# The last expert's scatter accumulates in PSUM on sums loaded there, and the norm chain reads the banks

## What is computed

```python
out = jnp.zeros((T + 1, D), jnp.float32).at[slot_tok].add(ys.astype(jnp.float32) * slot_gate[:, None])   # moe_ffn: 32 experts, 4 per token
...
x = x + gt2 * rms_norm(y, g_post_ffn[l])            # end of first_block
...
y = x * rsqrt(mean(x * x) + EPS) * norm_mix_gain    # start of second_block, rmsnorm
proj = y @ w_in_2
```

## Time and profile before

| | us |
|---|---|
| median of 3 runs | 2637.76 |
| lowest, highest run | 2636.64, 2644.43 |
| profiled execution, its span | 2643.0 |
| TensorE granted clock, mean | 0.979 |
| PE busy | 2496.3 (94%) |
| DVE busy | 1329.3 (50%) |
| ACT busy | 913.3 (35%) |
| GpSimd busy | 261.3 (10%) |

### The profile page before, as it was taken

One profiled execution on the slowest core, in us unless ns is written; L12 is line 12 of the kernel. 1 busy time (PEld: TensorE's weight loads), 2 busy tenths in 40 slices (PEclk: granted clock), 3 DMA queues, 4 the chain that ended last, 5 costly groups with the idle time before them and its releaser, 6 DMA issues.

```text
span 2643.0 us, 39144 instructions
## 1 busy us (share of the span) xinstructions
PE 2496.3 (94%) x16618; PEld 1762.0 (67%) x16618; DVE 1329.3 (50%) x1846; ACT 913.3 (35%) x1243; POOL 261.3 (10%) x181
## 2 busy tenths in 40 slices
PE   7988999999989999879999999999999999999998
PEld 5652323333323333278899899998899999887997
DVE  4451222212223222188777755756665765785755
ACT  4441111111111111056555544553444444435443
POOL 3000000000000000021000101262011201202200
PEclk9999999999999999989999999999999999999999
DMA  9689999999999999953455566555466466451562
GB/s 335 212 311 425 427 428 406 427 428 427 428 423 414 427 428 428 427 182 132 152 199 192 183 207 208 178 172 191 163 223 208 159 208 207 136 171 38 177 210 103
DMA packets 248986, 713.68 MB, mean 270 GB/s; under 512 B 12563, under 2 KB 186345, under 8 KB 223910
## 3 DMA queue, kind: packets, MB, share of 16 engines
q1 hardware_dynamic: 237424, 690.26, 68.8%
q10 hardware_dynamic: 9446, 15.97, 1.8%
q0 software_dynamic: 1936, 4.87, 0.6%
HBM read 710.01 MB, written 1.05 MB: 269 GB/s over the span
## 4 chain that ended last, share of the span: by engine, by line
PE 51%; DVE 3%; ACT 2%; issue 1%; POOL 0%; DVEq 0%; ACTq 0%; POOLq 0%
PE bank L429 19%; PE bank L671 13%; PE bank L434 10%; PE bank L623 4%; PE bank L703 2%; ACT ap L3945 1%; PE bank L899 1%; PE bank L2680 1%; PE bank L3456 0%; PE bank L467 0%; DVE stats L3219 0%; DVE xa L3217 0%; PE bank L4025 0%; ACT hi L362 0%; PE bank L3759 0%
## 5 line engine op out<-in xcount | busy, mean ns | idle before, releaser
L371 DVE TENSOR_TENSOR lo<-ring,hi 128x2048 fp32r<-128x2048 f32 x251 | 601.8, 2403 | 249.1 <-ACT hi L362 248.8
L362 ACT ACTIVATE hi<-ring 128x2048 fp32r<-128x2048 f32 x251 | 476.0, 1900 | 136.3 <-PE bank L671 106.8
L2130 PE MATMUL bank<-expert,xg 128*64 128x512 f32 x1664 | 387.6, 604 | 29.0 <-DMA expert<-in_w_mlp 28.1
L429 PE MATMUL bank<-x_hi,hi 128*128 128x256 f32 (+1 forms) x1576 | 369.1, 279 | 0.0
L429 PE MATMUL bank<-x_lo,hi 128*128 128x256 f32 (+1 forms) x1576 | 366.7, 278 | 0.0
L429 PEld LDWEIGHTS bank<-x_hi,hi 128*128 128x128 f32 (+1 forms) x1576 | 296.1, 188 | 3.3 <-issue 1.8
L429 PEld LDWEIGHTS bank<-x_lo,hi 128*128 128x128 f32 (+1 forms) x1576 | 296.0, 188 | 2.2 <-issue 0.7
L2130 PEld LDWEIGHTS bank<-expert,xg 128*64 128x64 f32 x1664 | 114.0, 137 | 241.7 <-issue 208.0
L2260 DVE TENSOR_TENSOR acc<-bank,acc 128x512 f32<-128x512 f32 x100 | 62.1, 683 | 332.7 <-PE bank L2238 332.6
L434 PE MATMUL bank<-x_hi,lo 128*128 128x256 f32 (+1 forms) x1576 | 197.0, 278 | 0.9 <-DVE lo L371 0.9
L2213 PE MATMUL bank<-expert,aT 128*64 128x512 f32 x832 | 185.7, 596 | 5.5 <-DMA expert<-in_w_mlp 5.5
(11 more groups left out here) (697 smaller groups left out, 3908.5 us busy)
## 6 DMA issues: line engine op xcount, KB each, us to landing
expert<-in_w_mlp SPq DMA_DIRECT2D x192, 2048.0 KB, 18.9
ring<-in_l_ffn_w_in SPq DMA_DIRECT2D x88, 1024.0 KB, 5.1
ring<-in_l_ffn_w_out SPq DMA_DIRECT2D x44, 1024.0 KB, 4.9
ring<-in_w_ada SPq DMA_DIRECT2D x24, 1024.0 KB, 7.0
ring<-in_l_gm_w_in SPq DMA_DIRECT2D x24, 1024.0 KB, 5.2
ring<-in_ffn_w_up SPq DMA_DIRECT2D x22, 1024.0 KB, 5.1
ring<-in_w_in SPq DMA_DIRECT2D x21, 1024.0 KB, 7.4
ring<-in_l_gm_w_out SPq DMA_DIRECT2D x12, 1024.0 KB, 4.9
```

The costliest lines, as they stand in the source:

```text
L362: e.activation(k.half("hi", u), k.slot(j), ACT.Copy).then_inc(*k.up("hi_done"))
L371: e.tensor_tensor(k.half("lo", u), k.slot(k.units[u][0]), k.half("hi", u).bitcast(F32), SUB).then_inc(*k.up("lo_done"))
L429: e.matmul(o, l, r, start=fresh, stop=False, skip_group_check=True)
L2130: i = e.matmul(banks[n][j][h * CAP:(h + 1) * CAP, :], x, W[:, (2 * h + j) * 512:(2 * h + j + 1) * 512], start=c == 0, stop=False, skip_gro ...
```

## The change

- In the 33rd place the addition of expert 30 to `acc` is marked quarter by quarter. Between the two halves of expert 31's second product PE now multiplies the identity by the four quarters of `acc`, 128x128 by 128x512 in fp32, each into a bank of its own (`sums_begin_pe`).
- Expert 31's scatter adds to these banks (`sums_end_pe`). Its eight products go in two sides of four, the left 256 columns of each bank and then the right ones, with a wait of PE for its own left side between them.
- DVE's four additions L2248, its statistics and products, GpSimd's two products and a DVE memset go away. `chain_act` and `chain_dve` do the norm from the four banks, in both engines' programs behind the branch past the overflow.
- The waits of ACT and DVE for PE's end of the experts stand behind the chain, and no longer ahead of it.
- In the overflow body the addition goes to the banks, through a scratch tile `s_out`.

```diff
--- before.py
+++ after.py
@@ -2246,9 +2246,6 @@
             av = k.t["acc"][:, :, q * 256:(q + 1) * 256]
             e.wait_ge(*k.mm("back", n, q))
             e.tensor_tensor(av, two(k.got("back", n, q)[:, :]), av, ADD).then_inc(*k.DVE(frees=("back", n, q)))
-            if key and q % 2:
-                for b in range(2):
-                    k.mark("dve_done", *key, b, q // 2)
         return
     for b in range(2):
         for h in range(2):
@@ -2258,6 +2255,32 @@
                 e.tensor_copy(av, bank).then_inc(*k.DVE(frees=("back", n, b, h)))
             else:
                 e.tensor_tensor(av, bank, av, ADD).then_inc(*k.DVE(*((*key, b, h) if key else ()), frees=("back", n, b, h)))
+
+
+def sums_begin_pe(k, e):
+
+    for b, h in quarters():
+        bank = k.bank(e, "sum", "acc", b, h, hold=True)
+        e.wait_ge(*k.dve("acc", b, h))
+        e.matmul(bank[:, :], k.cc("ident"), quarter(k.t["acc"], b, h), start=True, stop=False, skip_group_check=True)
+
+
+def sums_end_pe(k, e):
+
+    t, n = k.t, OF[NE - 1][0]
+    e.wait_ge(*k.act("Y", n))
+    for side in range(2):
+        if side:
+            e.wait_ge(*k.mm("sum", "left", 1, 1))
+        for b, h in quarters():
+            rows = slice((2 * h + side) * 32, (2 * h + side + 1) * 32)
+            e.matmul(k.got("sum", "acc", b, h)[:, side * 256:(side + 1) * 256], t[f"G{n % 5}"][rows, b * 128:(b + 1) * 128], t[f"Y{n % 3}"][rows, 0:256],
+                     start=False, stop=True, skip_group_check=True).then_inc(*k.MM("sum", "acc" if side else "left", b, h))
+    acc_free(k, "sum")
+
+
+def sum_bank(k, b, h):
+    return k.got("sum", "acc", b, h)[:, :]
 
 
 SMALL_AT = 18
@@ -2297,6 +2320,8 @@
         if p >= 1:
             downs = {n: k.bank(e, "down", n, hold=True) for n in OF[p - 1]}
             for i in range(2):
+                if i and p == NE:
+                    sums_begin_pe(k, e)
                 down_pe(k, e, p - 1, i, downs)
             for n in OF[p - 1]:
                 k.release("down", n)
@@ -2305,8 +2330,7 @@
                 for j in range(UPS[n]):
                     k.release("up", n, j)
     past = over_count(k, e)
-    for n in OF[NE - 1]:
-        scatter_pe(k, e, n)
+    sums_end_pe(k, e)
     for flag in PE_:
         k.mark(flag, "meet", "experts")
     return past
@@ -2349,7 +2373,7 @@
                 mark_dve(k, e, n)
         if p >= 2:
             for n in OF[p - 2]:
-                scatter_dve(k, e, n)
+                scatter_dve(k, e, n, *(("acc",) if p == NE else ()))
         if p == LATE_AT:
             turned_dve(k, e)
         if p == B2_AT:
@@ -2359,7 +2383,6 @@
                 gate_dve(k, e, n)
         if p == SMALL_AT:
             small2_dve(k, e)
-    e.memset(k.t["moments"][:, :, 2:3], EPS).then_inc(*k.DVE())
     k.mark("dve_done", "meet", "experts")
     return over_count(k, e)
 
...
@@ -2477,7 +2499,6 @@
                     e.wait_ge(*k.at("slow_dve_done", x, h, j, "x"))
                     e.activation(t["s_th"], t["s_x"], ACT.Tanh, scale=0.851).then_inc(*k.up("slow_act_done", x, h, j))
         e.wait_ge(*k.at("slow_dve_done", NE - 1, "down", 1, 1))
-    met(k, e, "experts", of=PE_)
     k.past("act", "overflow")
 
 
...
+    k.past("dve", "overflow")
+
+
+def moe_out_act(k, e):
+    chain_act(k, e, "post2", lambda b, h: sum_bank(k, b, h), lambda b, h: k.mm("sum", "acc", b, h), "mix2")
     met(k, e, "experts", of=PE_)
-    k.past("dve", "overflow")
-
-
-def moe_out_act(k, e):
-
-    t, mv = k.t, k.t["moments"]
-    e.activation(t["warm"], k.cc("ident")[:, 0:1], ACT.Sqrt).then_inc(*k.ACT())
-    for b in range(2):
-        e.wait_ge(*k.dve("post2", "var", b))
-        e.activation(mv[:, b, 1:2], mv[:, b, 1:2], ACT.Sqrt, bias=mv[:, b, 2:3]).then_inc(*k.ACT("post2", "std", b))
-    k.mark("act_done", "meet", "post2")
-    rms_squares_act(k, e, "mix2", lambda b, h: k.dve("post2", "x", b, h))
-    met(k, e, "post2")
-
-
-def moe_scaled(k, e, b, h, inc):
-    e.tensor_tensor(quarter(k.t["unit"], b, h), quarter(k.t["acc"], b, h), k.t["g2"][:, h * 512:(h + 1) * 512], MUL).then_inc(*inc)
-
-
-def moe_out_pool(k, e):
+
+
+def moe_out_dve(k, e):
+    e.wait_ge(*k.pool("g2", "done"))
+    chain_dve(k, e, "post2", lambda b, h: sum_bank(k, b, h), k.t["g2"], "mix2", lambda b, h: ("sum", "acc", b, h))
     met(k, e, "experts", of=PE_)
-    for h in range(2):
-        e.wait_ge(*k.dve("acc", 1, h))
-        moe_scaled(k, e, 1, h, k.POOL("post2", "scaled", h))
-
-
-def moe_out_dve(k, e):
-
-    t, mv, acc, st = k.t, k.t["moments"], k.t["acc"], k.t["post2_stats"]
-
-    def stats(b, h):
-        e.bn_stats(st[:, b, h, :], quarter(acc, b, h)).then_inc(*k.DVE())
-
-    def mean_square(b):
-        e.wait_ge(*k.dve())
-        e.bn_aggr(mv[:, b, 0:2], st[:, b, :, :].rearrange("p a b -> p (a b)")).then_inc(*k.DVE())
-        e.wait_ge(*k.dve())
-        e.scalar_tensor_tensor(mv[:, b, 1:2], mv[:, b, 0:1], mv[:, b, 0:1], mv[:, b, 1:2], MUL, ADD).then_inc(*k.DVE("post2", "var", b))
-
-    def add(b):
-        inverse_dve(k, e, "post2", b)
-        e.wait_ge(*k.dve())
-        for h in range(2):
-            if b:
-                e.wait_ge(*k.pool("post2", "scaled", h))
-            e.scalar_tensor_tensor(quarter(t["xa"], b, h), quarter(t["unit"], b, h), mv[:, b, 1:2], quarter(t["xa"], b, h), MUL, ADD).then_inc(*k.DVE("post2", "x", b, h))
-
-    for n in OF[NE - 1]:
-        scatter_dve(k, e, n, "acc")
-    e.wait_ge(*k.dve())
-    for b in range(2):
-        for h in range(2):
-            stats(b, h)
-        mean_square(b)
-    e.wait_ge(*k.pool("g2", "done"))
-    for h in range(2):
-        moe_scaled(k, e, 0, h, k.DVE())
-    for b in range(2):
-        add(b)
-    meet(k, e, DVE_, "post2")
-    square_dve(k, e, "mix2", 0)
-    rms_unit_dve(k, e, "mix2", 0)
-    square_dve(k, e, "mix2", 1)
-    rms_unit_dve(k, e, "mix2", 1)
 
 
 def lay_moe(k, c):
...
@@ -4270,7 +4240,6 @@
     meet(k, e, POOL_, "post1")
     late_gate_pool(k, e)
     meet(k, e, POOL_, "experts")
-    moe_out_pool(k, e)
     meet(k, e, POOL_, "post2")
     e.wait_ge(*k.dve("mix2", "unit", 1, 1))
     decay_pool(k, e, "hg", k.t["hD"])
```

More of the change, by code:

```diff
@@ L2431, in over_banks @@
 def over_banks(k):
-    n = OF[NE - 1][0]
-    back = {k.of["back", n, q] for q in range(4)}
-    return [k.ps[i] for i in range(8) if i not in back]
+    sums = {k.of["sum", "acc", b, h] for b, h in quarters()}
+    return [k.ps[i] for i in range(8) if i not in sums]
 def overflow_pe(k, e, past):
@@ L2513, in overflow_dve @@
                 for b in range(2):
-                    av = t["acc"][:, b, hf * 512:(hf + 1) * 512]
+                    av = sum_bank(k, b, hf)
                     e.wait_ge(*k.at("slow_mm_done", x, "down", hf, b))
-                    e.scalar_tensor_tensor(av, ps[2 + b][:, :], t["gov"][:, b, x:x + 1], av, MUL, ADD).then_inc(*k.up("slow_dve_done", x, "down", hf, b))
+                    e.wait_ge(*k.at("slow_dve_done"))
+                    e.tensor_scalar(t["s_out"], ps[2 + b][:, :], t["gov"][:, b, x:x + 1], None, MUL).then_inc(*k.up("slow_dve_done"))
@@ L2517, in overflow_dve @@
+                    e.wait_ge(*k.at("slow_dve_done"))
+                    e.tensor_tensor(av, av, t["s_out"], ADD).then_inc(*k.up("slow_dve_done", x, "down", hf, b))
         e.wait_ge(*k.at("slow_dve_done", NE - 1, "down", 1, 1))
-    met(k, e, "experts", of=PE_)
     k.past("dve", "overflow")
 def moe_out_act(k, e):
-    t, mv = k.t, k.t["moments"]
-    e.activation(t["warm"], k.cc("ident")[:, 0:1], ACT.Sqrt).then_inc(*k.ACT())
-    for b in range(2):
-        e.wait_ge(*k.dve("post2", "var", b))
-        e.activation(mv[:, b, 1:2], mv[:, b, 1:2], ACT.Sqrt, bias=mv[:, b, 2:3]).then_inc(*k.ACT("post2", "std", b))
@@ L2573, in moe_out_dve @@
-    e.wait_ge(*k.pool("g2", "done"))
-    for h in range(2):
-        moe_scaled(k, e, 0, h, k.DVE())
-    for b in range(2):
-        add(b)
-    meet(k, e, DVE_, "post2")
-    square_dve(k, e, "mix2", 0)
-    rms_unit_dve(k, e, "mix2", 0)
-    square_dve(k, e, "mix2", 1)
-    rms_unit_dve(k, e, "mix2", 1)
+    e.wait_ge(*k.pool("g2", "done"))
+    chain_dve(k, e, "post2", lambda b, h: sum_bank(k, b, h), k.t["g2"], "mix2", lambda b, h: ("sum", "acc", b, h))
+    met(k, e, "experts", of=PE_)
 def lay_moe(k, c):
@@ L2614, in lay_moe @@
             k.t[f"ab{i}"], k.t[f"Y{i}"] = share[:, i * 1024:i * 1024 + 512], share[:, i * 1024 + 512:(i + 1) * 1024]
-        bi("post2_stats", 128, 2, 2, 6)
         k.t["s_act"] = share[:, 0:2048].rearrange("p (a b) -> p a b", a=KC)
-        k.t["s_x"], k.t["s_th"] = share[:, 2048:2304], share[:, 2304:2560]
+        k.t["s_x"], k.t["s_th"], k.t["s_out"] = share[:, 2048:2304], share[:, 2304:2560], share[:, 2560:3072]
 RG = (("rg_w_r_2", "BD0", "r", 15), ("rg_w_i_2", "BD1", "ig", 18))
```

## The result

Over 20 runs each the changed kernel takes 2642.17 us in the median and the kernel before 2636.80. The ratio is 1.0018, with a 95% interval from 1.0011 to 1.0026: slower by 0.18%, 4.7 us of 2637, within the 0.3% that I had set as the limit of "the same". The profiled execution of the changed kernel spans 2641.7 us. Single executions of either kernel lie several us beside their median (2631.33 to 2645.14 before, 2638.18 to 2645.03 after), as much as the effect; so what follows compares places inside the traces, all counted from one event, the start of the first half of expert 31's second product (L2209; 1122.75 us before, 1120.29 after). It comes ahead of the new products; over all fourteen traces, of either kernel, it lies between 1119.2 and 1123.1, so times counted from the program's start would mix in up to 4 us of spread from before the seam.

A forecast was written before the change was run, and what follows sets the result against it. PE's work and the holes in it bound the kernel, so the turning's start decides. The late copy of 1.5 us and what follows came to +4.2, plus 0.1 for waits: +4.3, 2642.0 us; own range 2640.5 to 2643.5.

The forecast's parts named there:

- Where the bound lies: At the turning (L467): its start decides, and everything behind it, PE-bound from 1150 on, moves with it.
- The sums are loaded, +1.5: PE between the halves of expert 31's second product: four identity products take 3.4 us, delaying the second half 1.5 us.
- The scatter in two sides, 1.9: Expert 31's scatter on PE: first bank whole 1.9 us after its start, costing nothing if ACT comes later.
- ACT's place, the stall of 4.9: ACT behind its overflow branch: a 4.9 us stall, then the table load, puts the first square at 1137.2.
- The chain, 9.15: Second norm from the banks: 9.15 us from first square to turning, putting the turning 4.2 us later.
- What is removed: DVE's additions and statistics and GpSimd's products: already counted in DVE's 11.80 us; GpSimd's going saves nothing more.
- DVE branches as before: DVE's overflow branch: unchanged; before, its 6.2 us stall was covered by the wait for the last weights.
- The first rival: ACT is ready when the banks are: turning 0.6 us sooner, time 2637.2 us; chance 0.12.
- My rival on the other side: ACT stalls a second time between branch and squares: another 4.9 us, +9.2 in all, 2647.0 us; chance 0.04.
- The clock: PE's return to full clock moves with the work, costing nothing; rival, one stretch late: +1.7 us, 2643.7; chance 0.08.
- The waits moved, +0.1: ACT between its root and the weight splits: two more waits add 0.1 us, bounds 0 and 0.24.
- The sum: Whole kernel: +4.2 and +0.1 give +4.3 us, median from 2637.76 to 2642.0 us, 0.16% more.

The follow-up runs named there:

- e11: Changed kernel without the overflow on any engine and without the four products of the identity; one run, no ratio given, turning at +17.3 us.
- e7: Changed kernel without the overflow on any engine (its branches, loads of the count and body left out); 0.9990 of the kernel before.
- e1: Changed kernel with ACT's load of the count, its branch and its part of the overflow left out; 1.0009 of the kernel before.
- e4: Changed kernel with ACT's branch ahead of its last copy, which stands in both paths; 1.0009 of the kernel before.
- e8: Changed kernel with only DVE's branch and its part of the overflow left out; one run, no ratio given, turning at +24.8 us.
- e12: The changed kernel itself measured once more; 1.0018 of the kernel before.
- e3: Changed kernel with the small activation that loads the Sqrt table moved ahead of ACT's load of the count and branch; 1.0031 of the kernel before.
- e10: Kernel before with ACT's first weight split moved into its hole ahead of the second norm's squares; 0.9990 of the kernel before.
- e5: Changed kernel with ACT's branch ahead of its last copy and DVE's ahead of the addition of expert 30, both kept in both paths; 1.0009 of the kernel before.
- e2: Kernel before with ACT's load of the count and its branch left out; 0.9995 of the kernel before.

## Why the prediction was right, point by point

*Where the bound lies.* Right: the start of the turning decides, and what is behind it follows at its distance (gain 4.5 us behind, both before and after).

*The sums are loaded, +1.5.* Measured 1.78 in the profile (5.50 - 3.72), and 2.1 between e11 and e7. From the first of the four products to the second half passed 3.64 us (1125.79 - 1122.15), against 3.4, and they began 0.1 us later than I had put them: my term was small by 0.3.

*The scatter in two sides, 1.9.* Measured 1.96 in e1. It cost nothing in the changed kernel.

*ACT's place, the stall of 4.9.* The mechanism was right, and shown by taking the stall away (e1, e7) and by moving it (e4). Its size was short: 6.2 in the profile, 5.6 and 5.8 in e8 and e12, 5.8 in e3. This is the largest miss, 1.3 us of the 1.9 by which the turning came later than I had worked out. The stall is no constant: e10, in all this the kernel before, had 5.8 too, so the 1.3 us are in good part the spread of the stall and not the change's. What sets its length is not shown. A packet of instructions comes in q14 some 3 to 4 us behind the branch (1132.2 behind 1128.6 in the changed kernel), and the next step some 1.5 to 2 us behind the packet's end, while the weights of the projection are loading (DMA share 1.02 until 1129); no run branched with the DMA queues empty, or past a shorter body.

*The chain, 9.15.* Measured 9.49 in the changed kernel, 9.46 in e8, 9.13 in e5. Of the difference 0.4 us stand between DVE's fulfilled wait (1136.9) and its first product (1137.38); it is in e3 and e12 too, where DVE's branch stands in its old place, and not in e5. e7, with 9.49, has its hole elsewhere, 0.46 us behind the second pair of products, and so have e8 and e11; in these three DVE has no branch. I leave both open.

*What is removed.* Right: the chain from the banks is shorter than the old one from DVE's first addition, 9.5 against 11.80, and e7 shows that this pays exactly for the later copy and the two-sided scatter, turning 19.4 against 19.4. By the turning the change wins nothing even with no stall in it; by the time e7 (0.9990) is not told apart from the kernel before.

*DVE branches as before.* Here a step failed, under cover. I had counted one stall for DVE, ending at +7; it has two, the second until +12.8. The first rival, with ACT ready in time, would therefore not have been 0.6 us faster than before: e1 and e4 are that case, and their turning is 1.8 us later than before's. My rival on the other side, a second stall, was put on ACT, where none was seen; it was on DVE.

*The clock.* I let the return move along with the work. In the two profiled executions it moved by about 1 us (from 1151.0 - 1122.75 = 28.3 to 1149.7 - 1120.29 = 29.4 us from the first half's start) while the work moved by 6.1, so the first products of the projection ran at full clock. At the projection's second group of products 4.3 of the 6.15 us are left: PE won back 1.8, a little more than the 1.7 that I had given as a bound.

```profile
1152.72 1.98 PE L623 MATMUL bank<-a_hi,lo 128*128 128x256 f32 x16
...
1159.97 0.28 PE L429 MATMUL bank<-a_hi,hi 128*128 128x256 f32 x1
```

That is the kernel before, and this the changed one:

```profile
1154.57 1.98 PE L623 MATMUL bank<-a_hi,lo 128*128 128x256 f32 x16
...
1160.38 2.10 PE L623 MATMUL bank<-a_hi,lo 128*128 128x256 f32 x16 [0.20 <-DVE lo L371]
...
1163.08 0.35 PE L429 MATMUL bank<-a_hi,hi 128*128 128x256 f32 x1 [0.61 <-ACT hi L362]
```

But at L429 5.6 us are left again ((1163.08 - 1120.29) - (1159.97 - 1122.75)): PE came early and had to wait for the next splits of DVE and ACT. ACT's next split starts 10.77 us behind the gain in both kernels (1157.33 - 1146.56, 1161.02 - 1150.25), whatever PE does. So not all behind the turning was PE-bound, as I had said; a faster PE is caught there by ACT.

Nor is the place of the return a property of the kernel. In e2, the kernel before in all but ACT's branch, with its turning at +19.2, the clock is back at +22.4 and the whole projection runs at the full level; in e10, with its turning at +19.4, at +25.1; over the fourteen traces it is between +22.2 and +29.4. What decides it is not shown, and what I read from one pair of executions must not be taken for the change's.

*The waits moved, +0.1.* The gain stands 4.52 us behind the turning, 4.45 before.

*The sum.* +4.3 predicted; 6.1 at the turning, 5.6 at the first product of L429, 5.4 by the medians, 4.7 by the ratio, whose interval reaches from 2.9 to 6.9. The prediction lies inside it; the terms were short by 0.3, 1.3 and 0.3, and the trace of one execution is not the mean of the runs. That the predicted median, 2642.0, falls within 0.2 us of the measured 2642.17 is luck: the kernel before had been put at 2637.76 from three runs and is at 2636.80 over twenty, and the shift that I took was 1.1 us too small, which cancels. The lower end of my own range does not follow from its terms either: with a stall of 4.0 and a late copy of 1.4 they give 2641.0 and not 2640.5.

## What to carry to other kernels

In this kernel a branch past the 32 written-out experts cost its engine 4.9 to 6.2 us behind it on ACT and DVE and 5.6 to 7.3 on PE, and DVE nearly the same again a little later; whether a shorter body costs less was not tried. Before work is moved from one engine to another, look which of the two stands behind such a branch, and what covered it until now. Such a branch can be put ahead of the engine's last piece of work, with that piece in both paths. And when a chain of engines is rebuilt, compare from the last shared event to the first one that the next stage waits for: here a chain 2.3 us shorter started later by as much, even with every stall gone.

## What the hardware showed that I had not expected

DVE stalls twice, each time until a packet of instructions has come: 5.6 and 5.1 us in e5, with a short branch, not taken, between the two, and in e1, with no second branch, until 11.8 us after the branch. The Trainium skill, Runtime: NRT & Kernel Launch, Instruction fetch mechanics, says that a taken branch out of the prefetched window waits for a DMA. The packets in q14 and the stalls on ACT and DVE agree with it, and the stall on PE is of the same kind by its length; the page gives no time for it, so what my prediction called agreement "in the size" was only that three engines stalled for microseconds. The Trainium skill, Advanced Engine Details and Errata, Control Flow Timing, gives about 108 ns for a compare-and-branch. The instruction itself took 50 to 72 ns on ACT and DVE, less than that, and neither figure says anything of what follows it.

Where a program is given its table loads matters as well: behind the branch the program loads a table anew, even when the one that serves squares and roots (in the changed kernel one load serves both) was loaded 6 us before (e3).
